# Hybrid SSD and differential attention layer: order of the score matmuls, place of the conv transposes, of the gate's sigmoid and of dt's transposes

## The reference

```
h = RMSNorm(x)
[z | xBC | dt | q | k | v | g_ssm | g_att] = h @ W_in
y_ssm = Mamba2(z, xBC, dt) @ W_ssm_proj      (8 groups of 8 heads of 64, one chunk of 256)
y_att = DiffAttn(q, k, v) @ W_attn_proj      (16 heads, each two softmaxes of 64-wide q and k)
x = x + (sigmoid(g_ssm) * y_ssm + sigmoid(g_att) * y_att) @ W_out
x = x + SwiGLU(RMSNorm(x))
```

## Time and profile before

| | us |
|---|---|
| median of 3 runs | 2143.59 |
| lowest, highest | 2143.51, 2145.18 |
| profiled execution, its own time | 2146.78 |
| its span, first to last instruction | 2145.1 |
| mean granted TensorE clock | 0.997 of full |

### The profile page before, as it was taken

How to read it: one execution, slowest core, us unless ns; L and a number is a source line. 1 busy time by engine, 2 the same in 40 slices (tenths; PEclk the granted TensorE clock), 3 DMA queues, 4 the chain that set the end, 5 groups by cost and what they waited for, 6 DMA issues and landing times.

```text
span 2145.1 us, 30393 instructions
## 1 busy us (share of the span) xinstructions
PE 2128.1 (99%) x10885; PEld 1802.7 (84%) x10885; DVE 1240.7 (58%) x1395; ACT 1021.0 (48%) x1290; POOL 136.3 (6%) x165
## 2 busy tenths in 40 slices
PE   9999999999999999999999999999999999999999
PEld 8888889877889888888888888888888888888887
DVE  6676445555766777777754455554554445544443
ACT  5444444555456555555554434454444444443332
POOL 1111000000001222222100000000000000000000
PEclk9999999999999999999999999999999999999999
DMA  6656654444456555555466555556656666555554
GB/s 221 206 177 208 202 178 147 137 152 132 165 186 211 185 176 177 180 180 176 157 186 235 187 190 189 188 187 188 191 187 190 187 193 187 186 192 201 196 204 139
DMA packets 206326, 394.56 MB, mean 184 GB/s; under 512 B 15601, under 2 KB 20386, under 8 KB 205746
## 3 DMA queue, kind: packets, MB, share of 16 engines
q1 hardware_dynamic: 203778, 385.00, 55.7%
q0 software_dynamic: 2336, 8.46, 1.3%
q10 hardware_dynamic: 144, 0.20, 0.0%
HBM read 387.24 MB, written 2.16 MB: 182 GB/s over the span
## 4 chain that ended last, share of the span: by engine, by line
PE 92%; DVE 3%; issue 3%; ACT 1%; DMA 0%; DVEq 0%; POOL 0%; SPq 0%; ACTq 0%; POOLq 0%
PE acc L1284 75%; PE acc L1298 11%; PE side L1314 2%; PE side L1386 2%; DVE w_lo L739 2%; PE side L1508 1%; DVE conv_x L849 1%; PE side L1389 0%; DVE yT L1018 0%; ACT w_hi L409 0%; DMA x_row<-in_x 0%; PE side L1514 0%; PE side L1462 0%; PE side L1404 0%; PE side L1406 0%
## 5 line engine op out<-in xcount | busy, mean ns | idle before, releaser
L739 DVE TENSOR_TENSOR w_lo<-w_raw,w_hi 128x1024 fp32r<-128x1024 f32 x712 | 901.1, 1270 | 788.1 <-ACT w_hi L409 784.5
L409 ACT ACTIVATE w_hi<-w_raw 128x1024 fp32r<-128x1024 f32 x712 | 753.5, 1060 | 1025.2 <-PE acc L1284 860.8
L1284 PE MATMUL acc<-w_hi,h_hi 128*128 128x512 f32 x896 | 356.0, 397 | 0.9 <-DVE w_lo L739 0.9
L1284 PE MATMUL acc<-w_hi,h_lo 128*128 128x512 f32 x896 | 350.4, 391 | 0.0
L1284 PE MATMUL acc<-w_lo,h_hi 128*128 128x512 f32 x896 | 350.3, 391 | 0.0
L1284 PE MATMUL acc<-w_hi,x2T_hi 128*128 128x512 f32 x704 | 274.9, 391 | 0.0
L1284 PE MATMUL acc<-w_hi,x2T_lo 128*128 128x512 f32 x704 | 274.1, 389 | 0.0
L1284 PE MATMUL acc<-w_lo,x2T_hi 128*128 128x512 f32 x704 | 273.9, 389 | 0.0
L1298 PE MATMUL acc<-h_hi,w_hi 128*128 128x256 f32 x768 | 223.2, 291 | 0.0
L1298 PE MATMUL acc<-h_hi,w_lo 128*128 128x256 f32 x768 | 217.2, 283 | 0.0
L1298 PE MATMUL acc<-h_lo,w_hi 128*128 128x256 f32 x768 | 217.1, 283 | 0.0
(11 more groups left out here) (224 smaller groups left out, 2393.9 us busy)
## 6 DMA issues: line engine op xcount, KB each, us to landing
w_raw<-in_w_in SPq DMA_DIRECT2D x320, 512.0 KB, 4.3
w_raw<-in_w_ffn_gate SPq DMA_DIRECT2D x88, 512.0 KB, 3.5
w_raw<-in_w_ffn_up SPq DMA_DIRECT2D x88, 512.0 KB, 3.5
w_raw<-in_w_ffn_down SPq DMA_DIRECT2D x88, 512.0 KB, 3.5
w_raw<-in_w_ssm_proj SPq DMA_DIRECT2D x64, 512.0 KB, 3.5
w_raw<-in_w_attn_proj SPq DMA_DIRECT2D x32, 512.0 KB, 4.3
w_raw<-in_w_out SPq DMA_DIRECT2D x32, 512.0 KB, 3.5
acs_b<-acs_scratch POOLq DMA_DIRECT2D x16, 512.0 KB, 6.4
```

The source lines that it names most:

```text
L409: nc.scalar.activation(w_hi[:, r], w_raw[:, r], ACT.Copy).then_inc(hi_ready, 1)
L739: nc.vector.tensor_tensor(w_lo[:, r], w_raw[:, r], w_hi[:, r].bitcast(F32), ALU.subtract).then_inc(lo_ready, 1)
L1284: done = nc.tensor.matmul(acc[p][:, t], a[:, k0 + kk, cut], w[:, r, kk], start=first and kk == n == 0, stop=last and kk == UK - 1 and n == 2)
```

## The change

Four edits, with some loops written out for them:

- The scores of a head start with the masks: one bf16 product of 384 columns (mask, zeros, mask) for each of the two banks, then the four score products on top of them, alternating between the lower and the upper 64 partitions. mask_b grows from 128 to 384 columns and moves; the setup fills it with three instructions instead of one.
- The gate stage stores g_att with ACT's Copy instead of Sigmoid; the sigmoid runs in place on ACT at unit 5 of each chunk of the projection by w_attn_proj, and DVE's product waits for it (gate_ready).
- dt's transposes move from before the first unit of that projection to behind its unit 0; DVE's first two steps of dt move to step 2 of chunk 0, its chain to step 5, and ACT's Exp to step 3.
- In the SSD groups the transposes of conv_x move from unit 3 to unit 4 of the z chunk; DVE does the second half of the decays at step 4 and xdt at step 5, and ACT copies y_row at step 5.

The diff, cut to its core:

```
@@ head_scores
                 for m in range(2):
-                    half = slice(m * DH, (m + 1) * DH)
-                    for q in range(TT):
-                        first, width = q * P, (q + 1) * P
-                        nc.tensor.matmul(side[:, 1 + m, first:first + width], qkT[half, 0, q * P:(q + 1) * P],
-                                         qkT[half, 1, 0:width], start=True, stop=False)
-
-                        last = nc.tensor.matmul(side[:, 1 + m, first + width - P:first + width], ident_b[:], mask_b[:],
-                                                start=False, stop=True)
+                    nc.tensor.matmul(side[:, 1 + m, 0:3 * P], ident_b[:], mask_b[:].rearrange("p n k -> p (n k)"), start=True, stop=False)
+                for q in range(TT):
+                    first, width = q * P, (q + 1) * P
+                    for m in range(2):
+                        half = slice(m * DH, (m + 1) * DH)
+                        last = nc.tensor.matmul(side[:, 1 + m, first:first + width], qkT[half, 0, q * P:(q + 1) * P],
+                                                qkT[half, 1, 0:width], start=False, stop=q == TT - 1)
                 last.then_inc(scores, 1)
@@ ACT, gate stage
-            with repeat(act, 2, [(unit, 2 * UPC)]) as i:
-                for c in range(2):
-                    chunk_with_heads(i * 4 + (8 + 2 * c))
-                    ours = merge_a[:, bass.ds(i * 2 + c, 1)].rearrange("p o t n -> p (o t) n")
-                    nc.scalar.activation(ours, acc[c][:], ACT.Sigmoid).then_inc(acc_free[c], 1)
+            for n in range(4):
+                chunk_with_heads(8 + 2 * n)
+                nc.scalar.activation(merge_a[:, n], acc[n % 2][:], ACT.Copy).then_inc(acc_free[n % 2], 1)
@@ ACT, attention projection
             act.wait_ge(dtT_sum, 1)
             nc.scalar.activation(dtT[:], side[0:HS, 1, 0:T], ACT.Copy).then_inc(dtT_ready, 1)
-            act.wait_ge(dt_u, 1)
-            nc.scalar.activation(soft[:, 2], soft[:, 1], ACT.Exp).then_inc(dt_exp, 1)
...
+                    if u == 5:
+
+                        nc.scalar.activation(merge_a[:, c], merge_a[:, c], ACT.Sigmoid).then_inc(gate_ready, 1)
+                    if c == 0 and u == 3:
+                        act.wait_ge(dt_u, 1)
+                        nc.scalar.activation(soft[:, 2], soft[:, 1], ACT.Exp).then_inc(dt_exp, 1)
@@ DVE, attention projection
+                    if c == 0 and u == 2:
+                        dt_logits()
+                    if c == 0 and u == 5:
+                        steps_of_dt()
+                chunk_done()
+                dve.wait_ge(gate_ready, c + 1)
+                gated = merge_a[:, c]
+                nc.vector.tensor_tensor(gated, acc[c % 2][:], gated, ALU.mult).then_inc(acc_free[c % 2], 1)
@@ PE, dt and attention projection
                 last.then_inc(dtT_sum, 1)
+
+            def dt_rows():
                 pe.wait_ge(dtT_ready, 1)
...
             def last_heads(u):
+                if u == 0:
+                    dt_rows()
...
-            with repeat(pe, 2, [(unit, 2 * UPC), (pair, 1)]) as i:
-                for c in range(2):
-                    chunk(rows_unit, c, ya_hi, ya_lo, between=last_heads)
+            chunk(rows_unit, 0, ya_hi, ya_lo, between=last_heads)
+            chunk(rows_unit, 1, ya_hi, ya_lo)
+            chunk(rows_unit, 0, ya_hi, ya_lo)
+            chunk(rows_unit, 1, ya_hi, ya_lo)
@@ DVE, z_chunk
                     if u == 4:
+                        decays(g, 1)
+                    if u == 5:
 
                         dve.wait_ge(xs_T, g + 1)
...
-                    if u == 5:
-                        decays(g, 1)
@@ ACT, z_chunk
-                    if u == 4:
+                    if u == 5:
 
                         act.wait_ge(xdt_ready, g + 1)
@@ PE, z_between
-                    if u == 3:
+                    if u == 4:
 
                         pe.wait_ge(xs_ready, g + 1)
```

More of the change, by code:

```diff
@@ L165, in layer @@
         ident_b = at("ident_b", 82, [P, P], BF16)
-        mask_b = at("mask_b", 82.25, [P, P], BF16)
+        mask_b = at("mask_b", 207, [P, 3, P], BF16)
         taps = at("taps", 82.5, [P, TAPS, XBC // P])
@@ L258, in layer @@
         x_normed, side_T, side_hi, side_lo = sem("x_normed"), sem("side_T"), sem("side_hi"), sem("side_lo")
-        ones_ready = sem("ones_ready")
+        ones_ready, gate_ready = sem("ones_ready"), sem("gate_ready")
         rows_T, cols_ready, setup_done = sem("rows_T"), sem("cols_ready"), sem("setup_done")
@@ L526, in _ @@
             nc.scalar.activation(wdt_hi[:], wdt[:], ACT.Copy).then_inc(wdt_hi_ready, 1)
-            with repeat(act, 2, [(unit, 2 * UPC)]) as i:
-                for c in range(2):
-                    chunk_with_heads(i * 4 + (8 + 2 * c))
-                    ours = merge_a[:, bass.ds(i * 2 + c, 1)].rearrange("p o t n -> p (o t) n")
-                    nc.scalar.activation(ours, acc[c][:], ACT.Sigmoid).then_inc(acc_free[c], 1)
+            for n in range(4):
+                chunk_with_heads(8 + 2 * n)
+                nc.scalar.activation(merge_a[:, n], acc[n % 2][:], ACT.Copy).then_inc(acc_free[n % 2], 1)
             act.wait_ge(dtT_sum, 1)
             nc.scalar.activation(dtT[:], side[0:HS, 1, 0:T], ACT.Copy).then_inc(dtT_ready, 1)
-            act.wait_ge(dt_u, 1)
-            nc.scalar.activation(soft[:, 2], soft[:, 1], ACT.Exp).then_inc(dt_exp, 1)
             act.wait_ge(pv, NA + STARTED)
-            with repeat(act, 2, [(unit, 2 * UPC)]) as i:
-                for c in range(2):
[L543 to L550, removed]
+            for c in range(4):
+                for u in range(UPC):
+                    split_hi()
+                    if u == 0:
+                        for n in range(CT):
+                            last = conv_first_taps(bc_raw[:, c * CT + n:c * CT + n + 1], c * CT + DI // P,
+                                                   bc[:, c * CT + n:c * CT + n + 1], n)
+                        last.then_inc(bc_first, 1)
+                    if u == 5:
[3 more added lines that the diff above has]
+                        nc.scalar.activation(soft[:, 2], soft[:, 1], ACT.Exp).then_inc(dt_exp, 1)
             act.wait_ge(acs_sum, 1)
@@ L772, in tables_and_lambda @@
                 nc.vector.tensor_copy(ident_b[:], ident)
-                nc.vector.tensor_copy(mask_b[:], mask_in[:]).then_inc(setup_done, 1)
+                nc.vector.memset(mask_b[:, 1], 0.0)
+                nc.vector.tensor_copy(mask_b[:, 0], mask_in[:])
+                nc.vector.tensor_copy(mask_b[:, 2], mask_in[:]).then_inc(setup_done, 1)
                 for n in range(2):
@@ L942, in _, with dt_logits @@
                     chunk_with_heads(i * 4 + (8 + 2 * c))
-            def steps_of_dt():
-                v, mag, u, p, s, s2 = (soft[:, n] for n in range(6))
+            v, mag, u_exp, p, s, s2 = (soft[:, n] for n in range(6))
+            def dt_logits():
                 by_tile = "p (t h) -> p t h"
@@ L951, in steps_of_dt @@
                 nc.vector.scalar_tensor_tensor(out=mag, in0=v, scalar=-1.0, in1=v, op0=ALU.mult, op1=ALU.min).then_inc(dt_u, 1)
+            def steps_of_dt():
                 dve.wait_ge(dt_exp, 1)
-                link(nc.vector.tensor_scalar(p, u, 2.0, None, ALU.add))
+                link(nc.vector.tensor_scalar(p, u_exp, 2.0, None, ALU.add))
                 link(nc.vector.reciprocal(p, p))
-                link(nc.vector.tensor_tensor(s, u, p, ALU.mult))
+                link(nc.vector.tensor_tensor(s, u_exp, p, ALU.mult))
                 link(nc.vector.tensor_tensor(s2, s, s, ALU.mult))
@@ L967, in steps_of_dt @@
                                                op0=ALU.mult, op1=ALU.mult).then_inc(dA_ready, 1)
-            steps_of_dt()
             nc.vector.tensor_tensor(after[:], ones[:], tri, ALU.subtract).then_inc(after_ready, 1)
[L973 to L990, removed]
+            for c in range(4):
+                for u in range(UPC):
+                    split_lo()
+                    if 1 <= u < TAPS:
+                        if u == 1:
+                            dve.wait_ge(bc_first, c + 1)
+                        for n in range(CT):
+                            last = conv_other_taps(bc_raw[:, c * CT + n], c * CT + DI // P, bc[:, c * CT + n], n, u)
+                        if u < TAPS - 1:
+                            link(last)
+                        else:
+                            last.then_inc(bc_conv, 1)
+                    if c == 0 and u == 2:
[6 more added lines that the diff above has]
+                nc.vector.tensor_tensor(gated, acc[c % 2][:], gated, ALU.mult).then_inc(acc_free[c % 2], 1)
             def tail_gated(g):
```

## The result

The changed kernel took 2109.74 us (median of 4 runs, 2109.3 to 2110.58) against 2143.67 before (4 runs); the ratio is 0.9834, 95% interval 0.9822 to 0.9846. That is 1.66% faster. The direction was right and 31.2 us of saving were forecast. The medians are 33.9 us apart, the two profiled executions 36.9 (2146.78 and 2109.88). What follows is about the traces, and so mostly about the missing 5.7 us.

The account below looks back on a forecast made before the run. TensorE was taken to bound the kernel, busy 2128.1 of 2145.1 us. Savings 16.2 + 7.1 + 0.6 + 7.3 = 31.2 from 2146.8 gave 2115.6, less 3.2 gave 2112.4 us; range 2109 to 2121.

Parts of the forecast that it names:

- the slacks of yT, xdt and w_lo behind dt's chain: Spare time before PE needs these DVE results: yT 1.6 us, xdt 8 us, w_lo at unit 10 of the projection 1.7 us.
- 3.2 us off at the end: Savings were summed against the profiled execution, 2146.78 us; the runs' median, 2143.59, was 3.2 lower, so 3.2 was subtracted.
- Scores, forecast 16.2: Score blocks of 16 heads: merged masks and one switch save 12.8 us, overlap of halves 3.4; bounds 3.3 to 19.6.
- in series: Four scores of a head one after another without a mask between: 1.28 us, within about 1.93 a head after the change.
- the upper bound of the overlap: Score passes of one array half running beside the other's: at most 0.43 us a head, of which 0.21 was taken.
- rival (b): Score blocks: full overlap of the halves, short passes too; 34.6 us saved, 2109.0 us; chance 0.10.
- Rival (c): Score blocks: each change of half drains, so the scores' 16.2 us becomes 3.3; 2125.3 us; chance 0.08.
- Rival (a): Score blocks: no overlap of halves, everything else as forecast; 27.8 us saved, 2115.8 us; chance 0.27.
- Sigmoid, forecast 7.1: Gate stage: moving the sigmoid out removes PE's exps and qkT waits and the slow clock, 7.1 us; bounds 5 to 7.1.
- Rival (e): Heads: four half-array scores in a row make the clock fall at every head; slower, about 2162 us; chance 0.03.
- Conv, forecast 7.3: Seven SSD groups: later conv transposes no longer wait for yT, 1.04 us each, 7.3 in all; bounds 5 to 7.3.
- dt, forecast 0.6: Attention projection: dt's transposes behind unit 0 no longer wait for the copy of dtT; 0.6 us saved.

Follow-up runs that it names:

- scores-alone kernel: The kernel before with only the new score block and its mask tile (masks first, halves alternating): 2120.66 us, ratio 0.9876.
- masks-after block: The changed kernel with two 128-column masks behind each pair of scores instead of two long masks first: 2112.61 us.
- same-half block: The changed kernel with both score matrices computed on the lower 64 partitions, leaving out the second softmax's own scores: 2120.18 us.
- halves-in-turn: The changed kernel with all scores of the lower half issued before all of the upper half: 2110.48 us.
- sigmoid back: The changed kernel with the gate's sigmoid back in the gate stage in place of ACT's Copy: 2113.65 us.

## Why the prediction was right and where it failed

- **Bound and places: right.** PE bounds; the four places were the ones, and every wait that was to go went. No new one came: the slacks of yT, xdt and w_lo behind dt's chain came out within 0.4 us of the forecast's.
- **The median inside the range: in part luck.** The sum took 3.2 us off at the end, because the profiled execution of before was that much above the median. The changed kernel's profiled execution (2109.88) is only 0.14 above its median. So the forecast was 5.7 us too high for the profiled execution and 2.7 for the median: 3 us of the missed saving are hidden by a correction that did not carry over. That these 3 us were falls of the clock, which the change took away, fits the clocks of the runs but is not shown, since the first runs of before have no clock on record.
- **Scores, forecast 16.2: the failed step.** The blocks gave 11.1 us over the first eight heads (127.6 us from the first to the ninth head's transposes became 116.5) and 1.39 a head in chunk 0 of the gate stage: 16 x 1.39 = 22.2 us in all; the scores-alone kernel has 21.2. The merged masks and the single switch were priced well (the masks-after block came out at 1.60 for 1.59, and the same-half block at 2.06, where "in series" had forecast about 2.05: 1.93 of PE's time and the 0.12 turn of the last projection matmul). Wrong was the upper bound of the overlap, 0.43 us a head, of which I took 0.21. I had chained the passes in program order, so that each could at best start with its predecessor, and had then let the weight loads come one after the other. The halves-in-turn and same-half kernels show neither: the halves run as two independent queues, loads included, and save the whole of the shorter queue, 0.65 a head. That is 16 x (0.65 - 0.21) = 7 us more. Some 1 us of it was lost again, most of it because the full-array work right behind the block now takes 0.02 to 0.05 us longer to get going: the block itself became 1.41 to 1.44 us shorter, the time up to the projection's second matmul behind it only 1.39. Even rival (b), full overlap at 2109.0, was built on that bound, which is why the low end sat too high.
- **Rival (c), a drain at each change of half:** refuted by every block above. Rival (a), no overlap: refuted by the same-half kernel.
- **Sigmoid, forecast 7.1: right as a reading, wrong as a share.** The stretches of the chunks gave back just these 7 us, and alone on the kernel before the edit is worth 6.4. But taken from the changed kernel it is worth 3.3. The 4.7 us of clock that I booked under it needed both the wait and the long block behind it. The sum is not spoiled by that, because the scores were priced without any clock.
- **Rival (e), the clock falling at every head:** it fell at none. With the shorter blocks it stayed up even behind waits of 1 us (scores alone, sigmoid back).
- **Conv, forecast 7.3:** 7.9, mis-sized by the ordinary length of one step (0.30 for 0.23).
- **dt, forecast 0.6:** 0.6.
- Together 22.2 + 7.1 + 7.9 + 0.6 = 37.8 against 37.1 in the trace; with the 6.4 of the sigmoid alone it is 37.1. Nearly all of the missing saving is the scores: 6.0 more than forecast, with 0.6 more from the conv transposes and 0.7 less from the sigmoid.

## What to carry to other kernels

Two fp32 products that contract over 64 rows, one on the lower and one on the upper partitions and with results in different banks, cost PE the time of one here, with nothing full-array between them; put masks before or behind the pair. When a stall is followed by a fall of the clock, price it as one event with two causes, and ask of each edit whether it alone removes it. And when the nearest rows bound an unknown from one order of instructions only, leave the bound open to the case where the order does not matter at all.

## What the runs showed of the hardware that I had not expected

- The two row halves of TensorE run as separate queues, for fp32 passes and their weight loads: eight passes in 0.93 us against 1.58 on one half, with the halves alternating or one half's four issued before the other's. The Trainium skill ("TensorE: Matmul & The Clock Gate", Part 3) lets matmuls in different row groups run together, and the trace agrees; it also calls the matmuls strictly first in, first out, which the halves-in-turn kernel with its unchanged block of 1.41 us does not bear out across halves.
- The clock did not fall after a 1 us wait alone (none of five in front of 1.4 us blocks, none of seven in front of full-array transposes), but did where long half-array work followed (2.7 us: two of two).
- Moving full-array work out from between half-array pieces saves more than its own time: four masks with 0.54 us a head (0.16, 0.16, 0.15 and 0.07 to the next start) became two that take 0.42 with the switch, yet the block lost 1.44: 0.65 by the overlap, and 0.59 because the scores no longer go over to the half array and back four times.
